# A decoder layer on one core: the first chunk's modulation columns made directly, partial products in another order, fewer filler transposes

## What is computed

```python
c_act = jax.nn.silu(c)
mod = c_act @ w_ada[l] + b_ada[l]                  # (1, 6 * 1024)
sh1, sc1, g1, sh2, sc2, g2 = [m[:, None, :] for m in jnp.split(mod, 6, axis=-1)]
h = rms_norm(x, g_pre_mix[l]) * (1.0 + sc1) + sh1
y = hybrid_mixer(h, w_in[l], ...)                  # begins with proj = h @ w_in
x = x + g1 * rms_norm(y, g_post_mix[l])
h = rms_norm(x, g_pre_ffn[l]) * (1.0 + sc2) + sh2
y = swiglu(h, w_up[l], w_down[l])
x = x + g2 * rms_norm(y, g_post_ffn[l])
```

## Time and profile before

| | |
|---|---|
| median of 3 runs | 456.76 us (456.65 to 457.12) |
| the profiled execution's own time | 456.9 us |
| its span in the trace | 455.2 us |
| PE busy | 440.2 us, 97% of the span |
| DVE busy | 330.7 us, 73% |
| ACT busy | 243.6 us, 54% |
| chain that ended last | PE 91%, DVE 4%, issue 2%, ACT 2%, DMA 1% |
| longest waits of PE | x by DMA 5.5 us; L1641 for DVE's low part 0.7; L1641 for ACT's high part 0.7; L1606 for ACT's row 0.4 |

### The profile page before, as it was taken

How to read it: one execution, slowest core, us unless ns; L and a number is a source line. 1 busy time by engine, 2 the same in 40 slices (tenths; PEclk the granted TensorE clock), 3 DMA queues, 4 the chain that set the end, 5 groups by cost and what they waited for, 6 DMA issues and landing times.

```text
span 455.2 us, 7884 instructions
## 1 busy us (share of the span) xinstructions
PE 440.2 (97%) x2966; PEld 388.9 (85%) x2966; DVE 330.7 (73%) x587; ACT 243.6 (54%) x432; POOL 35.1 (8%) x76
## 2 busy tenths in 40 slices
PE   5999999999999999999999999999999999999994
PEld 3678998999999899999997899888888888888883
DVE  4625659887898887866995785896696687677655
ACT  4413885565777755587554676443534525425332
POOL 2000102100322231000000001000000000000000
PEclk9999999999999999999999999999999999999998
DMA  8999376797688558745559516998748658530002
GB/s 291 383 377 341 115 257 200 278 303 261 233 286 308 157 185 313 237 140 194 181 224 351 203 49 194 371 314 268 234 157 291 201 184 275 185 138 0 1 0 92
DMA packets 61634, 99.86 MB, mean 219 GB/s; under 512 B 3892, under 2 KB 44452, under 8 KB 61604
## 3 DMA queue, kind: packets, MB, share of 16 engines
q1 hardware_dynamic: 56480, 81.57, 52.8%
q0 software_dynamic: 4960, 17.84, 11.2%
q10 hardware_dynamic: 164, 0.05, 0.0%
HBM read 98.40 MB, written 1.05 MB: 218 GB/s over the span
## 4 chain that ended last, share of the span: by engine, by line
PE 91%; DVE 4%; issue 2%; ACT 2%; DMA 1%; SPq 0%; DVEq 0%; ACTq 0%
PE psum L1579 17%; PE psum L1982 16%; PE psum L1580 16%; PE psum L1581 16%; PE psum L1983 8%; PE psum L1641 3%; PE psum L1929 3%; PE psum L1595 2%; PE psum L1768 1%; DVE wlo L1113 1%; DMA xt<-in_x_dram 1%; PE psum L1703 1%; PE psum L1701 1%; PE psum L1630 1%; PE psum L1750 1%
## 5 line engine op out<-in xcount | busy, mean ns | idle before, releaser
L1982 PE MATMUL psum<-hcut,whi 128*128 128x512 f32 x320 | 111.5, 392 | 0.0
L1983 PE MATMUL psum<-hcut,wlo 128*128 128x256 f32 x320 | 89.5, 280 | 0.0
L1579 PE MATMUL psum<-hcut,whi 128*128 128x256 f32 x280 | 82.1, 293 | 0.3 <-DVE wlo L1113 0.3
L1580 PE MATMUL psum<-hcut,whi 128*128 128x256 f32 x280 | 79.1, 283 | 0.0
L1581 PE MATMUL psum<-hcut,wlo 128*128 128x256 f32 x280 | 79.1, 282 | 0.0
L1113 DVE TENSOR_TENSOR wlo<-raw,whi 128x768 fp32r<-128x768 f32 (+3 forms) x68 | 64.4, 972 | 15.6 <-ACT whi L749 15.0
L1982 PEld LDWEIGHTS psum<-hcut,whi 128*128 128x128 f32 x320 | 59.9, 187 | 13.2
L1983 PEld LDWEIGHTS psum<-hcut,wlo 128*128 128x128 f32 x320 | 60.4, 189 | 0.3
L749 ACT ACTIVATE whi<-raw 128x768 fp32r<-128x768 f32 (+3 forms) x68 | 55.6, 850 | 6.4 <-PE psum L1893 3.2
L1579 PEld LDWEIGHTS psum<-hcut,whi 128*128 128x128 f32 x280 | 53.4, 191 | 5.5 <-ACT qk L829 1.8
L1580 PEld LDWEIGHTS psum<-hcut,whi 128*128 128x128 f32 x280 | 53.5, 191 | 0.0
(11 more groups left out here) (252 smaller groups left out, 830.8 us busy)
## 6 DMA issues: line engine op xcount, KB each, us to landing
raw<-in_w_up_dram SPq DMA_DIRECT2D x22, 1024.0 KB, 7.5
xn<-in_w_ada_dram POOLq DMA_DIRECT2D x32, 512.0 KB, 4.9
raw<-in_w_in_dram SPq DMA_DIRECT2D x6, 2048.0 KB, 8.9
draw<-in_w_down_dram SPq DMA_DIRECT2D x11, 1024.0 KB, 5.0
ada<-in_w_ada_dram SPq DMA_DIRECT2D x16, 384.0 KB, 9.3
raw<-in_w_in_dram SPq DMA_DIRECT2D x3, 1536.0 KB, 8.9
raw<-in_w_o_dram SPq DMA_DIRECT2D x8, 512.0 KB, 4.5
raw<-in_w_in_dram SPq DMA_DIRECT2D x3, 1280.0 KB, 7.2
```

What stands on the lines that cost most here:

```text
L1579: pe.matmul(dst, a[0], b[0], start=first, stop=False)
L1580: pe.matmul(dst, a[0], b[1], start=False, stop=False)
L1982: pe.matmul(dst[:, :], wh, hcut[:, k, :, :].rearrange("p a s -> p (a s)"), start=k == 0, stop=False)
L1983: mm = pe.matmul(dst[:, S:2 * S], wl, hhi[:, k, :], start=False, stop=k == KC - 1)
```

## The change

- In `row_products` of g = 0, each step first issues four more products: for both of its k and for a = 0 and 1, `ada[:, k, a, 0:P]` (128x128, float32) as the stationary factor and one column of `csil` moving, summed in bank 7. After p = 3 they are the first chunk's shift and scale sums, as columns, and raise `mod_first`. The row products of g = 0 leave the first chunk's 128 columns out and are 256 wide instead of 384.
- For g = 0 ACT's `keep_row(0, 0, 1)` and PE's `turn_first(0)` go away. The waits on `row_kept` are renumbered. The waits for `pick_ready` and `x_kept_act` move to `turn_others`, that for `x_kept_dve` to the first step.
- `warm_up` is called with 2, 2 and 2 instead of 6, 8, 8 and 4: 6 filler transposes instead of 26. None stands between step 0 and 1 any more.
- Chunks 1, 2, 4 and 5 are multiplied kind by kind in the order 0, 2, 1: the first kind waits only for `w_hi` and `chunk_hi`, kind 2 for `w_lo`, kind 1 for `chunk_lo`. Chunk 7 stays unit by unit.
- The places of the steps for g = 1 and 2 are now counted in products: (1, 28), (2, 13), (2, 17), (4, 15) and (5, 7) where they stood after 30, 15, 18, 18 and 9; the turnings at (2, 26) and (5, 19) where they stood after 27 and 21.

```diff
@@ def row_products(g, p)
                 if p == 0:
                     if g:
-                        pe.wait_ge(row_kept, 2 * g)
+                        pe.wait_ge(row_kept, 2 * g - 1)
                     else:
                         pe.wait_ge(c_ready, 2)
+                        pe.wait_ge(x_kept_dve, 1)
+                if g == 0:
+
+                    for k in (2 * p, 2 * p + 1):
+                        for a in range(2):
+                            mm = pe.matmul(bank[7][:, a:a + 1], ada[:, k, a, 0:P], csil[:, k:k + 1], start=k == 0 and a == 0,
+                                           stop=k == KC - 1, skip_group_check=True)
+                    if p == KC // 2 - 1:
+                        mm.then_inc(mod_first, 1)
+                c0 = 0 if g else P
                 for odd in range(2):
                     for a in range(2):
                         p0 = 64 * odd + 32 * a
-                        mm = pe.matmul(bank[5][p0:p0 + 32, 0:n], crep[:, 2 * p + odd, :], ada[:, 2 * p + odd, a, 0:n],
+                        mm = pe.matmul(bank[5][p0:p0 + 32, c0:n], crep[:, 2 * p + odd, :], ada[:, 2 * p + odd, a, c0:n],
                                        start=p == 0, stop=p == KC // 2 - 1, tile_position=(0, p0))
                 mm.then_inc(gemv, 1)
...
-            PRODUCTS_AT = {(1, 9): ((1, 0), (1, 1)), (2, 4): ((1, 2),), (2, 5): ((1, 3),), (4, 5): ((2, 0), (2, 1)), (5, 2): ((2, 2), (2, 3))}
-            TURN_ROW_AT = {(2, 8): 1, (5, 6): 2}
+            PRODUCTS_AT = {(1, 28): ((1, 0), (1, 1)), (2, 13): ((1, 2),), (2, 17): ((1, 3),), (4, 15): ((2, 0), (2, 1)), (5, 7): ((2, 2), (2, 3))}
+            TURN_ROW_AT = {(2, 26): 1, (5, 19): 2}
...
-            warm_up(6)
             row_products(0, 1)
-            warm_up(8)
+            warm_up(2)
             row_products(0, 2)
-            warm_up(8)
+            warm_up(2)
             row_products(0, 3)
-            turn_first(0)
-            warm_up(4)
+            warm_up(2)
...
                 pe.wait_ge(w_hi, 2 * (k + 1))
-                pe.wait_ge(w_lo, 2 * (k + 1))
                 pe.wait_ge(chunk_hi, k + 1)
-                pe.wait_ge(chunk_lo, k + 1)
-                for u in range(FIRST_UNIT):
-                    mm = first_unit(u, k)
...
+                for n, (i, u) in enumerate((i, u) for i in (0, 2, 1) for u in range(FIRST_UNIT)):
+                    if u == 0 and i == 2:
+                        pe.wait_ge(w_lo, 2 * (k + 1))
+                    elif u == 0 and i == 1:
+                        pe.wait_ge(chunk_lo, k + 1)
+                    mm = first_unit(u, k, (i,))
+                    if n == 3 * FIRST_UNIT - 1:
                         mm.then_inc(chunk_done, 1)
-                    for g, p in PRODUCTS_AT.get((k, u), ()):
-                        row_products(g, p)
-                    if (k, u) in TURN_ROW_AT:
-                        turn_first(TURN_ROW_AT[k, u])
-                        turn_others(TURN_ROW_AT[k, u])
+                    modulation_between(k, n + 1)
```

More of the change, by code:

```diff
@@ L874, in _ @@
                     n = PORTION[g + 1] - k
-                    keep_row(g, 0, 1)
                     if g:
+                        keep_row(g, 0, 1)
                         keep_row(g, 1, n)
@@ L1599, in turn_first, with turn_others @@
             def turn_first(g):
+                pe.wait_ge(row_kept, 2 * g)
+                pe.matmul(bank[7][:, 0:2], mrow[:, 0:P], pick[:, :], start=True, stop=True).then_inc(mod_first, 1)
+            def turn_others(g):
                 pe.wait_ge(row_kept, 2 * g + 1)
@@ L1604, in turn_first @@
                     pe.wait_ge(x_kept_act, 1)
[L1605 to L1610, removed]
                 for c in range(1, PORTION[g + 1] - PORTION[g]):
@@ L1822, in first_of_portion, with modulation_between @@
                 mm.then_inc(chunk_done, 1)
-            for k in range(KC):
+            def modulation_between(k, n):
+                for g, p in PRODUCTS_AT.get((k, n), ()):
+                    row_products(g, p)
+                if (k, n) in TURN_ROW_AT:
+                    turn_first(TURN_ROW_AT[k, n])
+                    turn_others(TURN_ROW_AT[k, n])
+            for k in range(KC - 1):
                 if k in PORTION:
@@ L1828, in _ @@
                 pe.wait_ge(w_hi, 2 * (k + 1))
-                pe.wait_ge(w_lo, 2 * (k + 1))
                 pe.wait_ge(chunk_hi, k + 1)
-                pe.wait_ge(chunk_lo, k + 1)
-                for u in range(FIRST_UNIT):
-                    mm = first_unit(u, k)
-                    if k == KC - 1:
-                        mm.then_inc(units, 1)
-                    elif u == FIRST_UNIT - 1:
-                        mm.then_inc(chunk_done, 1)
-                    for g, p in PRODUCTS_AT.get((k, u), ()):
-                        row_products(g, p)
-                    if (k, u) in TURN_ROW_AT:
-                        turn_first(TURN_ROW_AT[k, u])
-                        turn_others(TURN_ROW_AT[k, u])
+                for n, (i, u) in enumerate((i, u) for i in (0, 2, 1) for u in range(FIRST_UNIT)):
[5 more added lines that the diff above has]
+                    if n == 3 * FIRST_UNIT - 1:
+                        mm.then_inc(chunk_done, 1)
+                    modulation_between(k, n + 1)
+            k = KC - 1
+            pe.wait_ge(w_hi, 2 * KC)
+            pe.wait_ge(w_lo, 2 * KC)
+            pe.wait_ge(chunk_hi, KC)
+            pe.wait_ge(chunk_lo, KC)
+            for u in range(FIRST_UNIT):
+                first_unit(u, k).then_inc(units, 1)
             for u in range(FIRST_UNIT, N_UNITS):
```

## The result

The changed kernel is slower: 460.31 us (median of 6 executions, 457.95 to 461.11) against 456.69 (6, 456.07 to 457.12), a ratio of 1.007, 95% interval 1.005 to 1.009. I had forecast 454.4 and a range of 453.6 to 455.9.

The account below looks back on a forecast made before the run. PE was taken as the bound, with gains possible in its own time or before it has work. 1.4 + 0.4 + 0.1 + 0.4 + 0.2 - 0.2, unrounded 2.38, off 456.76 gave 454.4, range 453.6 to 455.9.

Parts of the forecast that it names:

- So I expect no fall: PE's clock in the start: the new gaps are far shorter than the pause that lowered it before, so no cost.
- the rival: In the start, the clock rises later, making the kernel slower from two steps on; chance 0.05 for one step, 0.08 for more.
- two steps late: Case of a late clock rise in the start's steps: 1.2 + 1.4 + 0.2 lost, 457.2; within the 0.08 chance.
- late into chunk 0: Case of the clock rising only in chunk 0: 4.3 on top, up to 461.5; within the 0.08 chance.
- First product: Start of chunk 0: first product at 17.23 instead of 18.61 through a shorter chain, gain 1.4.
- the column products cost more: Start's steps: 1.1 per step leaves a gain of about 1.0, chance 0.10; 1.52 leaves none, chance 0.05.
- ACT's cut as the other arm: Before the first product: ACT cuts the front piece until 16.44, independent of the change, which limits the gain to 1.5.
- The joints: Where chunks meet: 0.4 gained between 0 and 1, 0.4 between 3 and 4, earlier turnings 0.1 and 0.2.
- The kinds' price: Chunks multiplied kind by kind: another bank for each of 110 products costs 0 to 0.3, taken as 0.2.
- Turnings: Turning of the other columns in chunks 2 and 5: one and two products earlier, gains 0.1 and 0.2.
- The transfer of part 3 of portion 1: Rival before the first turning: the load lands a us later and PE waits, 455.4; chance 0.07.
- Something downstream: Rival after unit 10: something bound by time, not semaphores, gives the gain back, 456.8; chance 0.05.

Follow-up runs that it names:

- f2: The changed kernel with 128 equal moving columns in each column product instead of 1, 6 fillers: 455.13 us, repeated 455.04.
- a1: The changed kernel once more, no edit: 460.38 us; its traced execution 458.1.
- f1: The changed kernel with 32 equal moving columns in the column products and all 26 filler transposes: 459.19 us; traced execution 466.5.
- e2: The kernel before with 6 filler transposes instead of 26, no column products, no new order: 458.44 us, ratio 1.004.
- e3: The kernel before with only the order by kinds and the new places of the steps; rows, turning and fillers as before: 455.86 us, ratio 0.9971.
- e4: The changed kernel with 32 equal moving columns in each column product instead of one: 454.83 us, ratio 0.9949.
- b1: The changed kernel with 32 moving columns and 6 fillers, measured again: of six executions four at 454.0 to 455.8, two at 461.7.
- f3: The changed kernel with 128 equal moving columns in the column products and no filler transposes: 454.91 us, ratio 0.9957.

## Why the prediction was wrong
**Wrong step: "So I expect no fall".** The sum put the clock at nothing after the first step. What the runs show in its place is a low level that costs 3.9 us at unit 10 when it falls in the middle (57.86 against f2's 53.94) and 6.6 us when it stays low from the first step into chunk 0 (60.50), in 15 of 16 executions. I judged the clock by whether PE pauses: before, it lost the level only after PE's work had ended, and in the new start I found no long pause. In a1's trace it fell with PE busy in every us. What had changed was what runs through the array: eight records of one column behind 128x128 loads in each step. I had written that down as what speaks for the rival ("keep the array nearly empty") and didn't weigh it. That the number of moved columns matters is shown by the runs that change nothing else (1, 8, 32 and 128 columns: 15 of 16, 7 of 10, 2 of 10 and 0 of 12 over 457.9). By what rule the chip decides is not shown, nor why executions of one kernel differ.

**The rival was priced about right for the late rise.** 457.2 for two steps late, up to 461.5 for late into chunk 0; seen 460.1 to 461.1 in ten of 16, one of them traced. A low step takes 1.67 + 1.01 (9.80 to 11.47 to 12.48 in the trace at 460.88), against 1.5 + 1.0 in the sum. But 0.08 was its chance, and the range ended at 455.9, cutting off the only rival with another sign. The fall in the middle (five of 16, 458.0 to 458.4) had no price of its own; that it lies between those of the late rise is luck. In the trace of before, the first step's 1.50 against 0.85 showed a clock that had not come up yet at 11; a path that stood on its coming up was the place for a wide range.

**By the Trainium skill's rule** ("TensorE: Matmul & The Clock Gate", Part 4: transposes don't count as products do) I had drawn both that the fillers were useless and that the clock could rise later, and gave the second no more than the 0.13 of the rival. f1 is in line with the rule (22 transposes between 13 and 24 us didn't bring the level up), e2 doesn't fit it; no run here settles it.

**The sum, where the clock is held (f2), came out, in part by luck:**
- First product: 17.23 forecast, 17.17 in f2, 17.13 in the execution at 455.43. Two errors cancel here. Column products were too cheap in the sum: 0.88 to 0.99 for a step (11.38 to 12.37 in f2) and not 0.74, the narrowed rows 0.57 and not 0.50, some 0.9 together up to the last column product. And the first step, taken as cold, was mostly at the full level: step 1 begins at 11.38 and not at 12.4. With a first step as cold as in the earlier trace rows, the same chain with the measured sizes gives an estimate of 18.4 for the first product, a gain of 0.2 and not 1.4. The rival "the column products cost more" (priced at 1.1 a step) was thus half right.
- ACT's cut as the other arm: free at 16.33 in f2, forecast 16.44; scaling at 16.51, forecast 16.57. Right.
- The joints: 1.07 from the first product to unit 10 in e3 (37.87 against 36.80), 1.10 in f2 (53.94 - 17.17 = 36.77), forecast 1.00. The kinds' price of 0.2 is nearer to 0.1. Right.
- Turnings forecast at 31.4 and 44.8, in f2 at 31.46 and 44.68; unit 10 at 54.1, in f2 53.94.
- The end: f2's span is 453.0 and 452.8, forecast 452.8. Its ratio 0.9965 and 0.9953 gives 1.6 and 2.1 us, the sum said 2.4.
- The transfer of part 3 of portion 1 (chance 0.07): no wait in f2 or e3.
- Something downstream (chance 0.05): in five traces the shift at unit 10 stands in the span to 0.4 (+1.38 and +1.4; +4.02 and +4.0; -1.66 and -1.5; -2.54 and -2.2; -2.51 and -2.4). In others a part is lost later: -2.45 and -1.9 in e4, -1.89 and -1.1 in b1, -0.71 and 0.0 in e2, and f1's 3.0. So "what is won before 56.48 should arrive at the end" holds to within 0.8 us in an execution, f1 apart; the cause is open.

The version to keep is f2 or f3: the changed kernel with 128 equal moving columns: medians of 454.9 to 455.1, against 456.7 to 457.0 before on the same chips.

## What to carry to other kernels
Before filler work is taken out of the start, or small products are put in the place of wide ones there, ask at what clock that stretch runs and what raised it: where TensorE's clock has only just come up, a busy PE doesn't make the stretch safe. Where a product moves few columns behind a full stationary load, more moving columns can cost little (here some 0.1 us for eight records) and can keep the clock; here they turned a loss of 3.6 us into a gain of 1.6 to 2.1. And take more than four executions when the clock's state in one stretch can differ: four agreed here within 0.8 us, and of the next sixteen with that start five were 6 us or more slower and one 4.

## What the hardware showed that I had not expected
- TensorE fell from 2.4 to 1.2 GHz while the profile counted it busy in every us (a1, near 13), and stayed there for some 10 us, in a stretch of float32 products with one moving column, narrow rows and two transposes a step; it came back during chunk 0, whose products move 256 columns.
- The granted clock in the records is 1.00 before its first change even where the lengths are those of 1.2 GHz (1.71 for eight records at 19.22, 0.95 to 1.05 at the full level). The lengths of like instructions tell it, and the mean granted clock misleads: 0.985 at 458, 0.996 to 0.999 at 460 to 461.
- Eight float32 records behind 128x128 loads take 0.95 to 1.05 with 1 moving column, 0.98 to 1.08 with 32 and 1.06 to 1.16 with 128, at the full level.
- The same program meets its first step at either level: at the full one at 9.27 and 9.35, at the low one at 9.80, in three traces of the changed kernel.
